# Moving the softplus series of dt from VectorE to GpSimd in a two-block kernel, with the quotient taken through a power

## The chip, the cores and the metric

The kernel runs on one core of one Trainium2 chip. The metric is the device time of one launch in microseconds. Before the change three timed runs gave a median of 1166.14 us (1164.15 to 1167.24).

The engines have short names in the profile: PE is TensorE, PEld its weight loads, DVE is VectorE, ACT is ScalarE, POOL is GpSimd and SP is SyncE. Each engine works through its own queue in order; semaphores tie the queues together.

## The reference, cut to what matters

Two blocks of a transformer for 256 tokens of width 1024 in float32. The first block is a short convolution mixer, a latent attention mixer and two squared-relu layers. The second has a gated layer, a hybrid mixer (a state space part beside chunked attention) and a second gated layer. The change touches the step size of the state space part alone:

```python
dt = jax.nn.softplus(dt_raw.astype(jnp.float32) + dt_bias.astype(jnp.float32))
a = -jnp.exp(a_log.astype(jnp.float32))
...
xdt = (xf * dt[..., None]).reshape(bsz, nc, CHUNK, n_groups, m, hd)
a_cs = jnp.cumsum((dt * a).reshape(bsz, nc, CHUNK, n_groups, m), axis=2)
```

There are 16 heads, so dt is 256 tokens by 16 heads. On the chip that is 128 partitions by 32 columns (two tiles of 128 tokens, 16 heads each).

The kernel takes softplus(x) as max(x, 0) + log(1 + e) with e = exp(-|x|), and log(1 + e) as 2 (z + z^3/3 + ... + z^19/19) with z = e / (2 + e).

## The kernel before, in words

**Weights.** Every product takes its weights in slabs of 128 partitions by at most 2048 columns, through a ring of four places. SP loads a slab into `raw` as soon as the slab four before it has been split. ACT rounds it to `weight_hi` (`round_slab`, recorded at L591). DVE subtracts to get `weight_lo` (`split_slab`, recorded at L956); both of its inputs lie in SBUF. PE multiplies high by high, low by high and high by low (`up_product`, L1441 to L1443, 48 matmuls of 256 columns for a slab).

**The stage of the change.** It is the first part of the hybrid mixer in the second block. PE first makes v and dt (three slabs, `HV`), then six slabs of the convolution input (`HX`, j = 0 to 5), then four of queries and keys (`HQK`). The orders are written out by hand, one list for each engine:

- DVE takes dt_raw from PSUM and adds the bias (L1284), makes -|x| (L1286, L1287), splits one slab (the fourth of HX), works through the series (L1290 to L1304), and then for j = 0 to 5 does three taps of the causal convolution (L1313, six instructions: one input in PSUM, one in SBUF) and splits the slab four ahead. At j = 4 it also copies the running sums out.
- ACT takes exp(-|x|) (L850) and exp(a_log) (L852), then for each j the first tap with its bias (L869), the rounding of a slab, and the Silu of the convolution before it (L858, `conv_out`). After the last Silu it loads another function table and takes the exponentials of the running sums (L888, `decays`).
- PE, after the product of HX slab 3, waits for `adt`, the product of dt and a, which the series ends in. It then makes the running sums with four small matmuls (L1850 to L1853), and goes on with HX slabs 4 and 5 and the first slab of queries and keys. Then it waits for the fourth Silu and for `decays` before the transposes of L1870.
- POOL issues small loads (L535 to L537, and one of L487), and then waits for the running sums (L543).

Every small instruction of DVE and POOL whose result the next one reads goes through `then`: it counts up a semaphore and the engine waits for it. POOL's own work elsewhere is of the same kind: `root` (L492, L493) adds a constant and raises to the power -0.5 with `half_neg`, on one column, or on two at one place.

The values of dt and adt lie in `dt_work`, 10 rows of 32 columns inside `arena`, the name that the trace shows. dt itself is read by DVE at L1335.

Of the kernel before, what the change touches and what calls it, by code (L numbers as in the profile page):

```python
# [26 lines left out]
ALU = mybir.AluOpType  # L27
AX_X = mybir.AxisListType.X

P = 128  # L30
TOKENS = 256
TILES = TOKENS // P
# [20 lines left out]
SSD_HEADS, SSD_HD, SSD_GROUPS = 16, 64, 2  # L53
# [43 lines left out]
def two_blocks(nc, t, consts, out):  # L97
# [43 lines left out]
    with ExitStack() as ctx:  # L141
        def sb(name, shape, dt=F32):
            return ctx.enter_context(nc.sbuf_tensor(name, shape, dt))
# [32 lines left out]
        half_neg = sb("half_neg", [P, 1])  # L176
# [17 lines left out]
        def take(n, *dims):  # L194
            a = arena[:, at[0]:at[0] + n]
            at[0] += n
            if len(dims) == 2:
                a = a.rearrange("p (a b) -> p a b", a=dims[0])
            return a
# [26 lines left out]
        dt_work = take(10 * 32, 10, 32)  # L226
# [25 lines left out]
        class Sems:  # L252
# [5 lines left out]
            def __getitem__(self, n):  # L258
# [12 lines left out]
        hy = Sems("hy", "rows tap0 conv xbc dt_abs dt_exp adt qk_out v_out cum_ps cum_out cum_rows cum_kept cum_wide0 cum_wide1 decays "  # L271
                        "xs_ps xs_out y_skip xdt hank bias_ready cb_ps cb_act cb seg exp seg_w y_ps off_ps off_taken "
                        "y_sum z_gate y_gated sumsq rstd y_n y_ps_t y_hi y_lo")
# [11 lines left out]
        def spread(v, n):  # L285
            return v.rearrange("(a n) -> a n", a=1).to_broadcast([P, n])
# [4 lines left out]
        def heads(a, n=8):  # L291
            return a.rearrange("p (h d) -> p h d", h=n)

        def per_head(a, n=8):

            return a.unsqueeze(2).to_broadcast([P, n, SSD_HD])
# [165 lines left out]
        def _(pool):  # L462
# [22 lines left out]
            def norm_rows(b, *pairs):  # L485
                for dst, v, n in pairs:
                    pool.dma_start(dst, spread(v, n)).then_inc(norm[b]["rows"], 16)  # L487
# [49 lines left out]
            pool.dma_start(dskip_row, spread(t["d_skip_2"][0], SSD_HEADS)).then_inc(hy["rows"], 16)  # L537
            pool.wait_ge(norm[5]["tok"], 2 * TILES)
            norm_rows(6, (gain[:, :], t["ffn2_norm_2"][0], D))

            pool.wait_ge(hy["rows"], 64)
            pool.wait_ge(hy["cum_rows"], 1)
            pool.dma_start(cum_kept, rows[0:TILES * SSD_HEADS, :]).then_inc(hy["cum_kept"], 16)  # L543
            for g in range(4):
                tile, h = g // 2, g % 2
# [398 lines left out]
        def _(dve):  # L944
            steps = [0]
            vec = nc.vector

            def then(ins):

                steps[0] += 1  # L950
                ins.then_inc(dve_step, 1)
                dve.wait_ge(dve_step, steps[0])
# [5 lines left out]
            def split_slab(m):  # L958

                if m >= N_SLABS:  # L960
                    return
                dve.wait_ge(hi_done, m + 1)
                w = width[m]
                rest(weight_lo[:, m % RING, 0:w], raw[:, m % RING, 0:w], weight_hi[:, m % RING, 0:w])\
                    .then_inc(lo_done, 1)
# [85 lines left out]
            for c in range(SC_CHUNKS):  # L1051
# [8 lines left out]
                for back in (1, 2):  # L1060
                    for f in range(CT):
                        o = f * TOKENS
                        row = ROW_SC + (SC_TAPS - 1 - back) * KD + CT * c + f
                        ins = vec.scalar_tensor_tensor(
                            tmp_c[:, o + back:o + TOKENS], tmp_b[:, o:o + TOKENS - back], cols[:, row:row + 1],
                            tmp_c[:, o + back:o + TOKENS], ALU.mult, ALU.add)
# [209 lines left out]
            split_slab(HV + 1 + RING)  # L1276


            x_dt, neg_abs, e_dt, z_dt, z2_dt, series, dt, _, adt, exp_a = [dt_work[:, i, :] for i in range(10)]
            minus_adt = z_dt  # L1280
            dve.wait_ge(hy["rows"], 64)
            for tile in range(TILES):
                sl = slice(tile * SSD_HEADS, (tile + 1) * SSD_HEADS)
                ins = vec.tensor_tensor(x_dt[:, sl], acc[:, 2 * tile + 1, VDT // 2 - SSD_HEADS:VDT // 2], dtb_row, ALU.add)  # L1284
# [1 line left out]
            then(vec.tensor_scalar(neg_abs, x_dt, -1.0, None, ALU.mult))  # L1286
            vec.tensor_tensor(neg_abs, neg_abs, x_dt, ALU.min).then_inc(hy["dt_abs"], 1)  # L1287
            split_slab(HV + 2 + RING)
            dve.wait_ge(hy["dt_exp"], 2)
            then(vec.tensor_scalar(z_dt, e_dt, 2.0, None, ALU.add))  # L1290
            then(vec.reciprocal(z_dt, z_dt))
            then(vec.tensor_tensor(z_dt, z_dt, e_dt, ALU.mult))
            then(vec.tensor_tensor(z2_dt, z_dt, z_dt, ALU.mult))
            then(vec.tensor_scalar(series, z2_dt, 1.0 / 19, None, ALU.mult))
            for k in (17, 15, 13, 11, 9, 7, 5, 3):
                then(vec.scalar_tensor_tensor(series, series, 1.0 / k, z2_dt, ALU.add, ALU.mult))
            then(vec.scalar_tensor_tensor(series, series, 1.0, z_dt, ALU.add, ALU.mult))
            then(vec.tensor_scalar(dt, x_dt, 0.0, None, ALU.max))
            then(vec.scalar_tensor_tensor(dt, series, 2.0, dt, ALU.mult, ALU.add))
            for tile in range(TILES):  # L1300
                sl = slice(tile * SSD_HEADS, (tile + 1) * SSD_HEADS)
                ins = vec.tensor_tensor(minus_adt[:, sl], dt[:, sl], exp_a[:, 0:SSD_HEADS], ALU.mult)
            then(ins)
            vec.tensor_scalar(adt, minus_adt, -1.0, None, ALU.mult).then_inc(hy["adt"], 1)  # L1304

            for j in range(6):
                cy, ps = (tmp_a, tmp_b)[j % 2], up[j % 4]
                dve.wait_ge(hy["tap0"], CT * (j + 1))
                for back in (1, 2, 3):
                    for f in range(CT):  # L1310
                        o = f * TOKENS
                        row = ROW_XBC + (XBC_TAPS - 1 - back) * XT + CT * j + f
                        ins = vec.scalar_tensor_tensor(  # L1313
                            cy[:, o + back:o + TOKENS], ps[:, o:o + TOKENS - back], cols[:, row:row + 1],
                            cy[:, o + back:o + TOKENS], ALU.mult, ALU.add)
# [15 lines left out]
            for g in range(4):  # L1331
                tile, h = g // 2, g % 2
                dve.wait_ge(hy["xs_out"], g + 1)
                hd = tile * SSD_HEADS + 8 * h
                vec.tensor_tensor(heads(xdt[:, tile, h * HALF:(h + 1) * HALF]), heads(acc[:, g, :]),  # L1335
                                  per_head(dt[:, hd:hd + 8]), ALU.mult).then_inc(hy["xdt"], 1)
                if g == 1:
                    dve.wait_ge(hy["decays"], 1)
                    dve.wait_ge(hy["xdt"], 2)
                    vec.tensor_tensor(heads(xdt_end, SSD_HEADS), heads(xdt[:, 0, :], SSD_HEADS),  # L1340
                                      per_head(dt_work[:, 7, 0:SSD_HEADS], SSD_HEADS), ALU.mult).then_inc(hy["cb"], 1)
# [34 lines left out]
            for p in range(4):  # L1376
                g, tile = p % 2, p // 2
# [31 lines left out]
            for g in range(4):  # L1409
                tile, f = g // 2, g % 2  # L1410
# [580 lines left out]
```

## Time and profile before

| | |
|---|---|
| median of three runs | 1166.14 us (1164.15 to 1167.24) |
| the profiled execution, its own time | 1164.75 us |
| its span in the trace | 1162.9 us |
| PE busy | 1135.6 us, 98% of the span |
| DVE busy | 656.1 us, 56% |
| ACT busy | 514.4 us, 44% |
| POOL busy | 55.9 us, 5% |
| granted TensorE clock, mean | 0.995 of full |

Times in the trace are counted from the start of the span. The length of a matmul is from its start to the end of its drain, so starts are the better measure of PE's pace: in this stage they lie 0.12 us apart. Lines of a timeline merge instructions of one kind that follow each other (x6 is six of them, and the length is that of all). In square brackets stands the idle time of the engine before the line, and what ended it.

### The profile page before, as it was taken

Reading aid. Unit: us, or ns where it says so; the run is one execution under the profiler, and the core shown is the slowest. Engines: PE = TensorE matmul, PEld = TensorE weight load, DVE = VectorE, ACT = ScalarE, POOL = GpSimd, SP = SyncE. Lnnn points to the kernel's source line nnn. Section 1 sums busy time; section 2 is a strip of 40 time slices with the busy share of each in tenths; the row PEclk is TensorE's granted clock in tenths of the full one; section 3 lists DMA queues with packets and bytes.
Section 4 is the critical chain, followed back from the end, with each engine's and each line's share of the span. In section 5 each row is a group of like instructions: output and inputs, shape, how many; then the busy total and the mean of one; then the engine's idle time right before and its main releaser. Section 6 shows DMA issues by size and latency. Waiting matters only on the chain.

```text
span 1162.9 us, 18298 instructions
## 1 busy us (share of the span) xinstructions
PE 1135.6 (98%) x7542; PEld 1020.1 (88%) x7542; DVE 656.1 (56%) x736; ACT 514.4 (44%) x581; POOL 55.9 (5%) x103
## 2 busy tenths in 40 slices
PE   9999999999999999999999999999989999999997
PEld 7897999998886799999879999988987778999996
DVE  4756655555764664555474454446966765544553
ACT  4533444434445244444443434344636734443342
POOL 1000000000200000000010000001041011000000
PEclk9999999999999999999999999999989999999999
DMA  9654665554651476565544555565664153555641
GB/s 336 231 193 148 210 204 178 187 183 129 179 176 43 145 235 186 182 209 181 162 145 144 201 188 173 181 183 176 199 190 162 56 181 127 175 183 184 205 141 50
DMA packets 141627, 201.77 MB, mean 174 GB/s; under 512 B 9432, under 2 KB 119232, under 8 KB 141584
## 3 DMA queue, kind: packets, MB, share of 16 engines
q1 hardware_dynamic: 138208, 190.27, 50.7%
q0 software_dynamic: 3376, 10.90, 3.0%
q8 instruction: 31, 0.51, 0.2%
q14 instruction: 12, 0.10, 0.0%
HBM read 200.08 MB, written 1.06 MB: 173 GB/s over the span
## 4 chain that ended last, share of the span: by engine, by line
PE 86%; DVE 7%; ACT 3%; DMA 2%; issue 1%; POOL 1%; SPq 0%; DVEq 0%; POOLq 0%; ACTq 0%
PE up L1441 15%; PE up L1443 15%; PE up L1442 15%; PE acc L1474 11%; PE acc L1475 11%; PE acc L1477 11%; DVE weight_lo L956 2%; DMA raw<-in_sc_w_in 2%; ACT weight_hi L591 1%; PE acc L1547 1%; PE up L1518 1%; PE up L1791 1%; PE up L1529 1%; PE up L1463 1%; PE up L1467 1%
## 5 line engine op out<-in xcount | busy, mean ns | idle before, releaser
L956 DVE TENSOR_TENSOR weight_lo<-raw,weight_hi 128x2048 fp32r<-128x2048 f32 (+4 forms) x206 | 414.3, 2017 | 310.5 <-ACT weight_hi L591 310.3
L1441 PE MATMUL up<-xh,weight_hi 128*128 128x256 f32 x1548 | 440.8, 285 | 2.2 <-ACT cols L591 1.1
L591 ACT ACTIVATE weight_hi<-raw 128x2048 fp32r<-128x2048 f32 (+4 forms) x206 | 347.5, 1694 | 214.1 <-PE acc L1477 120.0
L1443 PE MATMUL up<-xh,weight_lo 128*128 128x256 f32 x1548 | 438.4, 283 | 0.0
L1442 PE MATMUL up<-xl,weight_hi 128*128 128x256 f32 x1548 | 438.4, 283 | 0.0
L1441 PEld LDWEIGHTS up<-xh,weight_hi 128*128 128x128 f32 x1548 | 297.4, 192 | 6.2 <-issue 1.7
L1442 PEld LDWEIGHTS up<-xl,weight_hi 128*128 128x128 f32 x1548 | 297.4, 192 | 2.7 <-issue 0.7
L1443 PEld LDWEIGHTS up<-xh,weight_lo 128*128 128x128 f32 x1548 | 297.2, 192 | 0.0
L1474 PE MATMUL acc<-weight_hi,hh 128*128 128x512 f32 x480 | 187.6, 391 | 0.6 <-DVE hl L956 0.6
L1475 PE MATMUL acc<-weight_lo,hh 128*128 128x512 f32 x480 | 187.5, 391 | 0.0
L1477 PE MATMUL acc<-weight_hi,hl 128*128 128x512 f32 x480 | 150.3, 389 | 0.0
L1477 PEld LDWEIGHTS acc<-weight_hi,hl 128*128 128x128 f32 x480 | 90.1, 188 | 19.2
L1474 PEld LDWEIGHTS acc<-weight_hi,hh 128*128 128x128 f32 x480 | 90.3, 188 | 18.8 <-issue 2.0
L1475 PEld LDWEIGHTS acc<-weight_lo,hh 128*128 128x128 f32 x480 | 90.3, 188 | 17.0
L678 ACT ACTIVATE tmp_a<-up 128x512 f32<-128x512 f32 x32 | 19.2, 599 | 120.7 <-PE up L1443 115.9
L1097 DVE TENSOR_TENSOR tmp_b<-tmp_a 128x512 f32<-128x512 f32 x32 | 22.2, 693 | 65.5 <-ACT tmp_a L678 65.5
L714 ACT ACTIVATE tmp_a<-up 128x512 f32<-128x512 f32 x22 | 13.2, 598 | 97.3 <-PE up L1443 93.2
L1474 PE MATMUL acc<-weight_hi,xh 128*128 128x256 f32 (+1 forms) x152 | 51.5, 339 | 1.3 <-DVE xl L956 1.3
L1475 PE MATMUL acc<-weight_lo,xh 128*128 128x256 f32 (+1 forms) x152 | 50.7, 333 | 0.0
L591 ACT ACTIVATE xh<-up 128x512 fp32r<-128x512 f32 (+1 forms) x43 | 22.7, 551 | 55.2 <-PE up L1529 43.0
L1477 PE MATMUL acc<-weight_hi,xl 128*128 128x256 f32 (+1 forms) x152 | 46.1, 333 | 0.0
L956 DVE TENSOR_TENSOR xl<-up,xh 128x512 fp32r<-128x512 f32 (+1 forms) x43 | 25.2, 630 | 27.5 <-ACT xh L591 27.2
(223 smaller groups left out, 856.7 us busy)
## 6 DMA issues: line engine op xcount, KB each, us to landing
raw<-in_ff_w SPq DMA_DIRECT2D x64, 1024.0 KB, 5.3
raw<-in_ffn_w_gate SPq DMA_DIRECT2D x22, 1024.0 KB, 5.4
raw<-in_ffn_w_up SPq DMA_DIRECT2D x22, 1024.0 KB, 5.4
raw<-in_ffn_w_down SPq DMA_DIRECT2D x44, 512.0 KB, 4.6
raw<-in_w_in SPq DMA_DIRECT2D x14, 1024.0 KB, 5.6
raw<-in_sc_w_in SPq DMA_DIRECT2D x11, 1024.0 KB, 7.5
raw<-in_w_out SPq DMA_DIRECT2D x6, 1024.0 KB, 5.0
raw<-in_sc_w_out SPq DMA_DIRECT2D x4, 1024.0 KB, 5.2
```

What stands on the lines that cost most here:

```text
L591: return nc.scalar.activation(dst, src, ACT.Copy, **kw)
L678: nc.scalar.activation(tmp_a[:, :], up[par][:, :], ACT.Relu).then_inc(q["relu"], 1)
L714: nc.scalar.activation(tmp_a[:, :], up[2 * par][:, :], ACT.Silu).then_inc(q["gate"], 1)
L956: return vec.tensor_tensor(dst, whole, high.bitcast(F32), ALU.subtract)
L1097: vec.tensor_tensor(tmp_b[:, :], tmp_a[:, :], tmp_a[:, :], ALU.mult).then_inc(q["squared"], 1)
L1441: mm(dst, w_h, xh[:, x_tile + k, :], start=first and k == 0, stop=False)
L1442: mm(dst, w_h, xl[:, x_tile + k, :], start=False, stop=False)
L1443: ins = mm(dst, w_l, xh[:, x_tile + k, :], start=False, stop=last and k == k_tiles - 1)
L1463: mm(dst, w_h[k], xh[:, k, :], start=k == 0, stop=False)
L1474: mm(d, s_h, h, start=first, stop=False, **open_group)
L1475: mm(d, s_h, l, start=False, stop=False, **open_group)
L1477: ins = mm(d, s_l, h, start=False, stop=last, **open_group)
```

## The change

The series of dt and its products go from DVE's queue to POOL's, where they stand behind the small loads and in front of the wait for the running sums. [...] The reciprocal of 2 + e becomes (2 + e)^-0.5, multiplied in twice. DVE keeps the bias and -|x|. PE's wait for `adt` stays where it is; DVE gets a wait for it ahead of the first product that reads dt (L1335).

```diff
             pool.wait_ge(norm[5]["tok"], 2 * TILES)
             norm_rows(6, (gain[:, :], t["ffn2_norm_2"][0], D))
+
+            x_dt, _, e_dt, z_dt, z2_dt, series, dt, _, adt, exp_a = [dt_work[:, i, :] for i in range(10)]
+            minus_adt = z_dt
+            gps = nc.gpsimd
+            pool.wait_ge(hy["dt_exp"], 2)
+            then(gps.tensor_scalar(z2_dt, e_dt, 2.0, None, ALU.add))
+            then(gps.tensor_tensor(z2_dt, z2_dt, half_neg[:, :].to_broadcast([P, 32]), ALU.pow))
+            then(gps.tensor_tensor(z_dt, e_dt, z2_dt, ALU.mult))
+            then(gps.tensor_tensor(z_dt, z_dt, z2_dt, ALU.mult))
+            then(gps.tensor_tensor(z2_dt, z_dt, z_dt, ALU.mult))
+            then(gps.tensor_scalar(series, z2_dt, 1.0 / 19, None, ALU.mult))
+            for k in (17, 15, 13, 11, 9, 7, 5, 3):
+                then(gps.tensor_scalar(series, series, 1.0 / k, None, ALU.add))
+                then(gps.tensor_tensor(series, series, z2_dt, ALU.mult))
+            then(gps.tensor_scalar(series, series, 1.0, None, ALU.add))
+            then(gps.tensor_tensor(series, series, z_dt, ALU.mult))
+            then(gps.tensor_scalar(series, series, 2.0, None, ALU.mult))
+            then(gps.tensor_scalar(dt, x_dt, 0.0, None, ALU.max))
+            then(gps.tensor_tensor(dt, series, dt, ALU.add))
+            for tile in range(TILES):
+                sl = slice(tile * SSD_HEADS, (tile + 1) * SSD_HEADS)
+                then(gps.tensor_tensor(minus_adt[:, sl], dt[:, sl], exp_a[:, 0:SSD_HEADS], ALU.mult))
+            gps.tensor_scalar(adt, minus_adt, -1.0, None, ALU.mult).then_inc(hy["adt"], 1)
 
             pool.wait_ge(hy["rows"], 64)
             pool.wait_ge(hy["cum_rows"], 1)
...
             vec.tensor_tensor(neg_abs, neg_abs, x_dt, ALU.min).then_inc(hy["dt_abs"], 1)
             split_slab(HV + 2 + RING)
-            dve.wait_ge(hy["dt_exp"], 2)
-            then(vec.tensor_scalar(z_dt, e_dt, 2.0, None, ALU.add))
-            then(vec.reciprocal(z_dt, z_dt))
-            then(vec.tensor_tensor(z_dt, z_dt, e_dt, ALU.mult))
-            then(vec.tensor_tensor(z2_dt, z_dt, z_dt, ALU.mult))
-            then(vec.tensor_scalar(series, z2_dt, 1.0 / 19, None, ALU.mult))
-            for k in (17, 15, 13, 11, 9, 7, 5, 3):
-                then(vec.scalar_tensor_tensor(series, series, 1.0 / k, z2_dt, ALU.add, ALU.mult))
-            then(vec.scalar_tensor_tensor(series, series, 1.0, z_dt, ALU.add, ALU.mult))
-            then(vec.tensor_scalar(dt, x_dt, 0.0, None, ALU.max))
-            then(vec.scalar_tensor_tensor(dt, series, 2.0, dt, ALU.mult, ALU.add))
-            for tile in range(TILES):
-                sl = slice(tile * SSD_HEADS, (tile + 1) * SSD_HEADS)
-                ins = vec.tensor_tensor(minus_adt[:, sl], dt[:, sl], exp_a[:, 0:SSD_HEADS], ALU.mult)
-            then(ins)
-            vec.tensor_scalar(adt, minus_adt, -1.0, None, ALU.mult).then_inc(hy["adt"], 1)
-
             for j in range(6):
...
                 hd = tile * SSD_HEADS + 8 * h
+                if g == 0:
+                    dve.wait_ge(hy["adt"], 1)
                 vec.tensor_tensor(heads(xdt[:, tile, h * HALF:(h + 1) * HALF]), heads(acc[:, g, :]),
```

## Rows read from the trace of the kernel before

**Rows 1.** The page: busy time of each engine, then the chain's shares.

```profile
PE 1135.6 (98%) x7542; PEld 1020.1 (88%) x7542; DVE 656.1 (56%) x736; ACT 514.4 (44%) x581; POOL 55.9 (5%) x103
...
PE 86%; DVE 7%; ACT 3%; DMA 2%; issue 1%; POOL 1%; SPq 0%; DVEq 0%; POOLq 0%; ACTq 0%
```

**Rows 2.** Timeline of DVE from 813 us: start, length, line, operation [idle before].

```profile
813.23 2.29 DVE L956 TENSOR_TENSOR weight_lo<-raw,weight_hi 128x2048 fp32r<-128x2048 f32 x1 [2.21 <-ACT weight_hi L591]
815.44 0.17 DVE L1290 TENSOR_SCALAR arena<-arena 128x32 f32<-128x32 f32 x1
...
819.58 2.68 DVE L1313 SCALAR_TENSOR_TENSOR tmp_a<-up,cols,tmp_a 128x255 f32<-128x255 f32 x6
822.17 2.28 DVE L956 TENSOR_TENSOR weight_lo<-raw,weight_hi 128x2048 fp32r<-128x2048 f32 x1
...
843.92 2.66 DVE L1313 SCALAR_TENSOR_TENSOR tmp_b<-up,cols,tmp_b 128x255 f32<-128x255 f32 x6
```

**Rows 3.** Timeline of ACT, at both ends of the stage.

```profile
811.18 0.20 ACT L852 ACTIVATE arena<-arena 128x16 f32<-128x16 f32 x1
...
839.15 1.02 ACT L869 ACTIVATE tmp_b<-up,cols 128x256 f32<-128x256 f32 x2 [1.84 <-PE up L1443]
...
846.61 0.63 ACT L858 ACTIVATE arena<-tmp_b 128x512 f32<-128x512 f32 x1 [4.11 <-DVE tmp_b L1313]
847.26 1.28 ACT L888 ACT_TABLE_LOAD   x1
```

**Rows 4.** Timeline of PE, at the wait for adt and at the transposes.

```profile
826.12 0.28 PE L1443 MATMUL up<-xh,weight_lo 128*128 128x256 f32 x1
826.33 0.41 PE L1850 MATMUL acc<-cst,arena 128*32 128x128 f32 x2
...
848.90 3.65 PE L1870 MATMUL acc<-cst,arena 128*128 128x128 f32 x16 [4.02 <-ACT arena L888]
```

**Rows 5.** Stages: us, busy of PE, PEld, DVE, ACT, POOL, granted clock, DMA share, GB/s.

```profile
845.00:849.00 4.00, 0.10 (x1) 0.14 (x2) 3.74 (x5) 2.36 (x4) 0.10 (x1) 0.82 0.88 250
849.00:852.00 3.00, 3.00 (x15) 3.00 (x16) 0.86 (x1) 3.00 (x5) 0.39 (x1) 0.50 0.64 152
852.00:855.00 3.00, 3.00 (x18) 3.00 (x17) 2.90 (x4) 1.10 (x3) 3.00 (x2) 0.60 0.70 213
```

**Rows 6.** Timeline of POOL: two columns, then one column, then its wait.

```profile
308.11 0.73 POOL L493 TENSOR_TENSOR rstd<-rstd,half_neg 128x2 f32<-128x2 f32 x1
...
589.76 0.19 POOL L525 TENSOR_TENSOR rstd<-mean_sq 128x1 f32<-128x1 f32 x1
590.04 0.22 POOL L492 TENSOR_SCALAR rstd<-rstd 128x1 f32<-128x1 f32 x1
590.35 0.57 POOL L493 TENSOR_TENSOR rstd<-rstd,half_neg 128x1 f32<-128x1 f32 x1
...
844.55 0.55 POOL L543 DMA_DIRECT2D cum_kept<-rows  x1 [52.65 <-DVE rows L1325]
```

**Rows 7.** POOL's four wide products: count, shortest/median/longest in ns, starts, form.

```profile
L548 POOL TENSOR_TENSOR normed<-normed,arena x4: 1034/1530/2726, 851.6 to 857.3; 128x512 f32<-128x512 f32 x4
```

**Rows 8.** Timeline of DVE, then of POOL, at 928 us.

```profile
928.22 4.49 DVE L956 TENSOR_TENSOR weight_lo<-raw,weight_hi 128x2048 fp32r<-128x2048 f32 x2
...
928.53 2.07 POOL L492 TENSOR_SCALAR rstd<-sumsq 128x1 f32<-128x1 f32 x1 [23.34 <-ACT bias L926]
930.68 2.46 POOL L493 TENSOR_TENSOR rstd<-rstd,half_neg 128x1 f32<-128x1 f32 x1
```

**Rows 9.** Timeline of DVE beside the one-column work of POOL in rows 6.

```profile
588.93 1.41 DVE L1015 SCALAR_TENSOR_TENSOR x_tok<-acc,mean_var,gain 128x512 f32<-128x512 f32 x2
590.38 0.75 DVE L1020 SCALAR_TENSOR_TENSOR x_tok<-x_tok,rstd,bias 128x512 f32<-128x512 f32 x1
```

**Rows 10.** Two products of DVE over 1024 columns, the first beside POOL's L548.

```profile
854.74 1.69 DVE L1340 TENSOR_TENSOR arena<-arena 128x1024 f32<-128x1024 f32 x1
...
927.09 1.22 DVE L1399 TENSOR_TENSOR normed<-normed,arena 128x1024 f32<-128x1024 f32 x1
```

More of the change, by code:

```diff
@@ L1276, in _ @@
             split_slab(HV + 1 + RING)
-            x_dt, neg_abs, e_dt, z_dt, z2_dt, series, dt, _, adt, exp_a = [dt_work[:, i, :] for i in range(10)]
-            minus_adt = z_dt
+            x_dt, neg_abs, dt = dt_work[:, 0, :], dt_work[:, 1, :], dt_work[:, 6, :]
             dve.wait_ge(hy["rows"], 64)
```

## The prediction

> **What bounds the kernel now.** I read the page first. PE is busy for 98% of the span and makes up 86% of the chain that ended last [rows 1], so a saving on DVE counts only where PE waits for DVE. I then read the timelines of the stage. From 815.44 us on DVE has no idle time: the series takes until 819.58, and six rounds of taps and a split follow, the last taps starting at 843.92 [rows 2]. A round is 2.6 us of taps and 2.2 us of split, 4.8 us (822.17 less 819.58, and the split's 2.28 less the overlap of starts). PE needs 48 matmuls x 0.12 = 5.8 us for a slab. DVE began late and catches up, but not wholly: the last taps end at 846.6, the last Silu follows at once, then a table load of 1.28 us [rows 3], and PE, idle for 4.02 us, starts its transposes at 848.90 [rows 4]. The stages show a second cost. The mean clock from 845 to 849 us is 0.82, so it fell to half (1.2 GHz) at about 847.6, 2.7 us after PE fell idle at 844.9; it is 0.50 until 852 and 0.60 from 852 to 855, so it rose at about 854.4 [rows 5]. PE worked from 848.9 to 854.4 at half speed, 5.5 us for 2.75 us of work.
>
> **What the removal is worth.** DVE loses 19 instructions, 819.58 - 815.44 = 4.14 us [rows 2]. I replayed the stage from 815.44 with the rows' lengths. The taps then start earlier, and from j = 3 on they wait for PE. PE's slab 5 is done where it was, and the first tap behind it starts at 839.15 as before [rows 3]. It lasts 1.0 us, the DVE taps until 842.7, Silu, table and exponential (0.6 + 1.28 + 0.2) until 844.9, and PE starts near 845.1 instead of 848.90: 3.8 us. Its idle time shrinks to some 0.2 us, so the clock has no idle time to fall in, which gives back 2.75 us. Together 6.6 us, if `adt` is there in time.
>
> **When adt is needed.** PE ends slab 3 at 826.12 + 0.12 = 826.24 and goes on at 826.33 [rows 4]: there is no wait now, since DVE's adt is there at 819.6. Behind that wait in PE's queue stand the running sums, slabs 4 and 5 and everything after. PE is the bound, so each us of lateness is paid in full.
>
> **What POOL needs.** The input is there when ACT's L852 ends, 811.4 [rows 3]; POOL has been idle since its small loads, 52.65 us in all [rows 6]. It gets 30 instructions: one addition, the power, and 28 more (13 with a constant, 15 with two tensors).
> - A small one of one column takes 0.19 us (two tensors) or 0.22 (constant), and the next starts 0.09 us later, 590.04 less 589.76 less 0.19 [rows 6]. For the columns I take the shortest L548, 1.034 us for 512 [rows 7]: (1.034 - 0.19)/511 = 1.65 ns a column, 0.05 us for 31. So 0.33 or 0.35 us each from start to start, 28 of them 15 x 0.33 + 13 x 0.35 = 9.5 us.
> - The power takes 0.57 us for one column and 0.73 for two [rows 6]: 0.16 us a column. For 32 that is 0.57 + 31 x 0.157 = 5.4 us. No row has more than two. Bounds: 0.6 us, if the second column's price is not repeated; 12.3 us, if each column costs what the first does above an addition, 0.19 + 32 x 0.38. I take 5.4, the only slope that a row shows.
>
> Undisturbed, adt comes at 811.4 + 0.35 + 5.4 + 9.5 = 826.7, almost in time. But POOL is disturbed. Two starts of DVE's split (both inputs in SBUF) fall at 928.22 and 930.42. POOL's addition, started at 928.53, lasts 2.07 us instead of 0.22 and ends at 930.60, just behind the first split; the power, started at 930.68, lasts 2.46 instead of 0.57 and ends 0.43 behind the second [rows 8]. So while a split runs POOL's next instruction stands, and one gets through for each. Beside L1015, with one input in PSUM and one in SBUF like the taps L1313, four of POOL's keep their 0.19 to 0.57 us [rows 6, 9]: the taps let POOL through. (The Trainium skill, SBUF — State Buffer, "Who interferes with whom", says this too: a VectorE instruction contends with a GpSimd one that reads SBUF when it has two SBUF inputs, not when it has one. The trace agrees: 2.07 against 0.22 us.)
>
> So each round of 4.8 us gives POOL the 2.6 us of taps: seven instructions, and the eighth stands until the split ends. Without the series DVE's splits lie at 813.2 to 815.4, 818.0 to 820.2, 822.8 to 825.0, 827.6 to 829.8 and 832.4 to 834.6. The power runs from 811.75 to 817.2, over the first of them. I take its reads as done by then. Three more start before 818.0, the fourth stands until 820.4; seven and one until 825.2; seven and one until 830.0; the last eight need 2.7 us, so adt comes at 832.7, or at 834.9 if the last falls into the split at 832.4. I take 833.8, a stall S of 7.5 us (6.5 to 8.7). Without the splits it would be 0.5 us.
>
> **The clock again.** An idle time of 7.5 us is longer than the 4.02 us in which it fell before. If it falls after 2.7 us again, that is at 829.0. Before, it stood at half for 6.8 us, 5.5 of them behind PE's new start. If the 6.8 us are what repeats, PE works at half from 833.8 to 835.8 and loses 1.0; if the 5.5, it loses 2.75. I take 2.0.
>
> **The sum.** PE starts its transposes S + 2.0 later than the 6.6 us of gain would have it: 7.5 + 2.0 - 6.6 = +2.9 us (bounds with S and the clock: 6.5 + 1.0 - 6.6 = +0.9 and 8.7 + 2.75 - 6.6 = +4.9). What follows the transposes hangs on PE and moves with it. Other edits at nothing: DVE's new wait at L1335 lies behind running sums that already need adt; behind POOL's new work stands L543, which waits for the same sums; with DVE earlier the slabs are loaded earlier, never later. The series' DVE time would have been hidden only where DVE has idle time, and that is not the case here.
>
> **Rivals.**
> 1. *A power whose price hardly grows with the columns* (0.6 us). It ends at 812.4; with the same blocking, adt comes at 827.7 to 830.0: a stall of 1.5 to 3.7 us, the clock lost or not: 6.6 less that, -5 to -0.2 us, middle 1162.6. Against it speaks the 0.16 us between one and two columns.
> 2. *A costly power, the other side: slower.* At 12.3 us it ends at 824.0. Nine instructions get through until 830.0, seven and one until 834.8, the other eleven run free, since DVE then waits for PE: 838.6, S = 12.4, and with 0 to 2.75 us of clock +5.8 to +8.6, middle 1173.3. It decides (over 0.3%) from S + clock = 10.1 us, a power of about 7 us.
> 3. *The power holds DVE's split back.* L1340, started 0.44 us after a wide product of POOL, takes 1.69 us instead of the 1.22 of L1399 [rows 10]: DVE waited 0.47. If the power keeps the way to SBUF for all its 5.4 us, the split of 813.23 starts at 817.1, DVE gains nothing, and the same count gives adt at 835.0: S = 8.8, +2.6 to +5.0, middle 1169.9. Against it: L1020, two inputs in SBUF, started 0.03 us after a power of one column and took its full-speed 0.75 us [rows 6, 9], so one column is not held through the arithmetic; with 32 no row tells. The Trainium skill, SBUF — State Buffer, "SBUF: two separate sides", says that the first to start gets the shared pair for the whole instruction. By that rule this rival is the forecast. Its sum would be +3.8 us where mine is +2.9.
> 4. *The splits don't hold 32-column instructions up as they did one-column ones.* adt at 826.7, S = 0.5, -6.1 us, 1160.0. Against: rows 8, twice.
>
> **How the numbers follow.** A difference under 0.3% (3.5 us) can't be told from none here. Chances: forecast 0.45, rival 1 0.13, rival 2 0.18, rival 3 0.20, rival 4 0.04. Slower by over 3.5 us come all of rival 2, half of rival 3 and a fifth of the forecast: 0.37. Faster come half of rival 1 and all of rival 4, and a little for what I overlook: 0.13. The rest, 0.50, is within 0.3%. The profiled execution took 1164.75 us for a span of 1162.9; the sum makes it 1167.7. The median of the runs lies 1.4 above it, so I predict 1166.1 + 2.9 = 1169.0. The range leaves out the tails of rivals 1 and 2: 1162.5 to 1174.0.
>
> **What the profile after would show.** The first taps of DVE at 815.5 (right) or 819 (rival 3). One POOL power of 128x32 near 5.4 us, the others near 0.25 us with some of 2 us under the splits. PE idle before L1850 for some 7 us, released by POOL, and a clock at half in that wait; no idle time of 4 us before L1870. The prediction is wrong if the power is far from 5.4 us, if small instructions of POOL have another price at 32 columns than at one, or if the taps hold POOL up too.

## The result, and the profile after

The changed kernel takes 1172.07 us (median; 1169.19 to 1172.81) against 1166.14 before, five runs each: a ratio of 1.0048, 95% interval 1.0031 to 1.0065. It is slower by half a per cent. The prediction said 1169.0, within 1162.5 to 1174.0, and gave "within 0.3%" the highest chance; the measured time lies in the range and past that bound, on the side that had 0.37.

The first view is the page of the changed kernel: busy time of each engine, then the chain's shares, as in [rows 1].

```profile
PE 1136.9 (97%) x7542; PEld 1021.2 (87%) x7542; DVE 652.6 (56%) x717; ACT 513.5 (44%) x581; POOL 77.0 (7%) x133
...
PE 86%; DVE 4%; ACT 3%; POOL 3%; DMA 2%; issue 1%; SPq 0%; DVEq 0%; POOLq 0%; ACTq 0%
```

DVE's share of the chain fell from 7% to 4% and POOL's rose from 1% to 3%. POOL got 21 us of busy time for the 3.5 us that DVE lost. In the listings that follow, the lines of the changed kernel are numbered 23 higher in ACT's part and 5 to 23 higher in DVE's and PE's.

POOL's timeline shows what the 21 us are (start, length, line, operation):

```profile
812.43 0.31 POOL L545 TENSOR_SCALAR arena<-arena 128x32 f32<-128x32 f32 x1 [21.16 <-ACT arena L875]
812.82 5.46 POOL L546 TENSOR_TENSOR arena<-arena,half_neg 128x32 f32<-128x32 f32 x1
818.36 0.26 POOL L547 TENSOR_TENSOR arena<-arena 128x32 f32<-128x32 f32 x1
818.70 0.25 POOL L548 TENSOR_TENSOR arena<-arena 128x32 f32<-128x32 f32 x1
819.02 2.33 POOL L549 TENSOR_TENSOR arena<-arena 128x32 f32<-128x32 f32 x1
...
824.00 2.21 POOL L552 TENSOR_SCALAR arena<-arena 128x32 f32<-128x32 f32 x1
...
828.77 2.23 POOL L552 TENSOR_SCALAR arena<-arena 128x32 f32<-128x32 f32 x1
...
833.22 2.51 POOL L561 TENSOR_TENSOR arena<-arena 128x16 f32<-128x16 f32 x2
835.82 0.29 POOL L562 TENSOR_SCALAR arena<-arena 128x32 f32<-128x32 f32 x1
```

And DVE's beside it, as in [rows 2]:

```profile
814.17 2.29 DVE L979 TENSOR_TENSOR weight_lo<-raw,weight_hi 128x2048 fp32r<-128x2048 f32 x1 [2.20 <-ACT weight_hi L614]
816.38 2.68 DVE L1318 SCALAR_TENSOR_TENSOR tmp_a<-up,cols,tmp_a 128x255 f32<-128x255 f32 x6
818.98 2.28 DVE L979 TENSOR_TENSOR weight_lo<-raw,weight_hi 128x2048 fp32r<-128x2048 f32 x1
...
823.77 2.29 DVE L979 TENSOR_TENSOR weight_lo<-raw,weight_hi 128x2048 fp32r<-128x2048 f32 x1
...
833.37 2.28 DVE L979 TENSOR_TENSOR weight_lo<-raw,weight_hi 128x2048 fp32r<-128x2048 f32 x1
846.35 2.68 DVE L1318 SCALAR_TENSOR_TENSOR tmp_a<-up,cols,tmp_a 128x255 f32<-128x255 f32 x6 [10.70 <-ACT tmp_a L892]
```

The taps start right behind the split of 814.17, as wanted. The power takes 5.46 us. Each of POOL's three instructions of 2.2 to 2.3 us began within 0.25 us of the start of a split and ended just behind it; the two of L561 are one more case, 2.51 us for both with the split of 833.37 beside them. The same operations take 0.25 to 0.3 us elsewhere. Behind the split of 833.37 DVE has 10.70 us of idle time: it waits, through ACT, for PE. PE's timeline and the stages with their clock show why (us, busy of PE, PEld, DVE, ACT, POOL, granted clock, DMA share, GB/s):

```profile
827.08 0.28 PE L1450 MATMUL up<-xh,weight_lo 128*128 128x256 f32 x1
836.16 0.64 PE L1857 MATMUL acc<-cst,arena 128*32 128x128 f32 x2 [8.81 <-POOL arena L562]
...
857.12 1.94 PE L1877 MATMUL acc<-cst,arena 128*128 128x128 f32 x16 [0.34 <-ACT arena L911]
```

```profile
830.00:834.00 4.00, 0.00 (x0) 0.00 (x0) 3.93 (x8) 0.73 (x2) 3.34 (x9) 0.58 0.63 175
834.00:838.00 4.00, 1.84 (x8) 1.45 (x9) 1.65 (x1) 0.00 (x0) 2.02 (x2) 0.50 0.74 206
838.00:842.00 4.00, 4.00 (x24) 4.00 (x25) 0.00 (x0) 0.00 (x0) 0.00 (x0) 0.64 0.64 219
```

The wait of 4.02 us before the transposes [rows 4] has become 0.34, and 16 transposes take 1.94 us instead of 3.65. In its place PE waits 8.81 us for POOL's last instruction, and the clock is at half from 830.6 (0.58 is 3.4 of 4 us at half) to 840.9 (0.64 is 2.9 of 4). PE works in the last 4.7 us of that and loses 2.35.

**A ruler for the stage.** The starts of a run differ by 1 to 3 us before the stage is reached, so I measure within it, in the one profiled execution of each kernel: from the start of the second exponential on ACT to the start of the first product behind the transposes (`bc_t`). Before and after:

```profile
859.00 0.59 PE L1877 MATMUL up<-arena 128*128 128x256 f32 x2
```

```profile
812.14 0.20 ACT L875 ACTIVATE arena<-arena 128x16 f32<-128x16 f32 x1
...
864.64 0.59 PE L1884 MATMUL up<-arena 128*128 128x256 f32 x2
```

Before it is 859.00 - 811.18 [rows 3] = 47.8 us, after it is 864.64 - 812.14 = 52.5. The stage costs 4.7 us more.

### The profile page after: what moved, and what is told of

The parts are those of the page before. It is cut to its first block, busy times and chain, and to the rows that moved or that the text cites. A ratio compares the mean times of both kernels' runs of the same rounds, so it can differ in the third digit from the quotient of the medians.

```text
span 1168.5 us, 18310 instructions
## 1 busy us (share of the span) xinstructions
PE 1136.9 (97%) x7542; PEld 1021.2 (87%) x7542; DVE 652.6 (56%) x717; ACT 513.5 (44%) x581; POOL 77.0 (7%) x133
## 4 chain that ended last, share of the span: by engine, by line
PE 86%; DVE 4%; ACT 3%; POOL 3%; DMA 2%; issue 1%; SPq 0%; DVEq 0%; POOLq 0%; ACTq 0%
PE up L1448 15%; PE up L1450 15%; PE up L1449 15%; PE acc L1481 11%; PE acc L1482 11%; PE acc L1484 11%; DMA raw<-in_sc_w_in 2%; PE acc L1554 1%; DVE weight_lo L979 1%; PE up L1525 1%; ACT weight_hi L614 1%; PE up L1536 1%; PE up L1798 1%; PE up L1470 1%; PE up L1474 1%
## 5 line engine op out<-in xcount | busy, mean ns | idle before, releaser
L1484 PE MATMUL acc<-weight_hi,xl 128*128 128x256 f32 (+1 forms) x152 | 46.1, 333 | 0.0
```

The lines of the kernel that those rows point to most:

```text
L1484: ins = mm(d, s_l, h, start=False, stop=last, **open_group)
```

## The experiments

Theory A is the prediction's: every us that adt comes behind PE's slab 3 is paid, with the clock that falls in the wait, and nothing else of the change costs. Its rivals stand in the expectations. All kernels but e4, e6 and e9 are edits of the changed kernel. "Stage" is the ruler above; "stall" is PE's wait for adt. The kernel before was run again beside each group of kernels, and each ratio is to those runs: their median was 1165.68 us beside e1 to e4, 1164.90 beside e5 to e8 and 1166.33 beside e9. The kernels e1 and e3 leave out the quotient and so don't compute dt; e2 leaves out terms of the series and computes it more coarsely.

| run | time, us | ratio to before, 95% interval | stall, us | stage, us |
|---|---|---|---|---|
| before | 1166.14 | | 0 | 47.8 |
| changed | 1172.07 | 1.0048 (1.0031 to 1.0065) | 8.81 | 52.5 |
| e1 no power | 1160.14 | 0.9944 (0.9927 to 0.9960) | 1.35 | 43.0 |
| e2 two terms | 1160.21 | 0.9946 (0.9930 to 0.9963) | 0.62 | 42.3 |
| e3 both short | 1161.02 | 0.9946 (0.9927 to 0.9965) | 0 | 41.6 |
| e4 ladder | 1165.93, one run | | 0 | 47.8 |
| e5 sums late | 1159.22 | 0.9954 (0.9940 to 0.9969) | 0 | 41.0 |
| e6 splits late, series on DVE | 1160.96 | 0.9962 (0.9949 to 0.9975) | 0 | 41.6 |
| e7 reciprocal on DVE | 1161.32 | 0.9963 (0.9949 to 0.9978) | 0.94 | 42.6 |
| e8 splits moved | 1165.64 | 1.0003 (0.9993 to 1.0012) | 2.97 | 46.1 |
| e9 sums late, series on DVE | 1165.73 | 1.0003 (0.9992 to 1.0013) | 0 | 46.4 |

The ruler and the ratios differ by up to 2 us, in both directions: e1 gains 4.8 us on the ruler and some 6.5 by its ratio, e6 gains 6.2 and some 4.4. So the order of e1, e2, e3, e6 and e7 among themselves is read from stall and stage, and the times show only that all five are faster than the kernel before.

**e1: no power.** The quotient is left out.

```diff
-            then(gps.tensor_scalar(z2_dt, e_dt, 2.0, None, ALU.add))
-            then(gps.tensor_tensor(z2_dt, z2_dt, half_neg[:, :].to_broadcast([P, 32]), ALU.pow))
+            then(gps.tensor_scalar(z2_dt, e_dt, 1.0, None, ALU.mult))
+            then(gps.tensor_tensor(z2_dt, z2_dt, half_neg[:, :].to_broadcast([P, 32]), ALU.mult))
```

> The quotient is left out: the first instruction and the power on GpSimd become plain multiplications, the other 28 instructions stay. Theory A (lateness: every us that adt comes after TensorE's slab 3 is paid, and nothing else of the change costs): the GpSimd chain loses 5.2 us of 5.46, but the splits of VectorE still stop it four times, so adt comes 5 to 7 us earlier than in the changed kernel. TensorE's stall falls from 8.8 us to 2 to 4 us, and the clock falls for a short time or not at all. Gain over the kernel before 6.6 less 2 to 4 less 0 to 2.4: 1160 to 1166 us, middle 1163. Theory B (the early start of the taps brings nothing, because the table load, the rounding or the loads set the transposes; the stall is all that counts): the kernel before plus the stall, 1168 to 1170 us.

The stall fell to 1.35 us, below the 2 to 4 that theory A expected, and the time to 1160.14, at the lower end of its range. adt came 7.5 us sooner, where 5 to 7 was expected, for 5.2 us of work less: three of POOL's instructions were held back by a split, and not four as I had written. Theory B, which wanted 1168 to 1170 us, is ruled out.

**e2: two terms.** Six of the eight middle terms of the series are left out.

```diff
-            for k in (17, 15, 13, 11, 9, 7, 5, 3):
+            for k in (5, 3):
```

> The power stays, six of the eight middle terms of the series are left out (k = 5 and 3 stay), so GpSimd runs 18 instructions instead of 30. Theory A: counted with seven free instructions for each round of taps and one held back by each split, adt comes about 8 us earlier than in the changed kernel, the stall is 0 to 1.5 us, the clock does not fall there, and the time is 6.6 less the stall below the kernel before: 1159.5 to 1161.5 us. Theory B: 1166 to 1168 us.

The stall is 0.62 us and the time 1160.21, as theory A has it.

**e3: both.** The two edits together.

> Both cuts together: no power and two of eight middle terms. adt is far ahead of TensorE's slab 3. Theory A: no stall there at all, the transposes start 3.8 us earlier than in the kernel before and at full clock, 1159.5 us (-6.6). It is the ceiling of what leaving the series off VectorE can bring. Theory B: equal to the kernel before, 1166 us.

adt is there 4.9 us ahead of PE. The stage takes 41.56 us where it took 47.82 before, 6.3 less; the prediction had 6.6 for a kernel without a stall. The median, 1161.02 us, is 1.5 above what was expected. The five runs of this kernel spread from 1157.89 us (mean clock 0.999) to 1162.64 (0.994), which is told below.

**e4: the ladder.** The kernel before, with unused work on POOL at the start.

```diff
+            then(nc.gpsimd.memset(ladder[:, :], 2.5))
+            for n in (1, 2, 4, 8, 16):
+                then(nc.gpsimd.tensor_tensor(ladder[:, 0:n], ladder[:, 0:n], half_neg[:, :].to_broadcast([P, n]), ALU.pow))
+            for n in (1, 16, 32):
+                then(nc.gpsimd.tensor_tensor(ladder[:, 0:n], ladder[:, 0:n], ladder[:, 32:32 + n], ALU.mult))
+                then(nc.gpsimd.tensor_scalar(ladder[:, 0:n], ladder[:, 0:n], 1.5, None, ALU.add))
```

> The kernel before with a ladder of instructions on GpSimd at the start of the program, where VectorE and GpSimd are idle: powers over 1, 2, 4, 8 and 16 columns, then a product and an addition over 1, 16 and 32 columns. If the price of the power is 0.57 us and 0.157 us for each further column: 0.57, 0.73, 1.04, 1.67, 2.92 us. If only the long one has such a slope, the short ones lie flatter. The small instructions: 0.19, 0.22, 0.24 us (product) and 0.22, 0.25, 0.27 us (addition) by the slope of the 512-column product; the changed kernel's rows say 0.25 and 0.29 at 32 columns. The time of the whole kernel is not changed by more than 3 us, as the ladder lies before the first load is used.

POOL's timeline of e4, four of the five powers and the small instructions of 32 columns:

```profile
1.82 0.56 POOL L479 TENSOR_TENSOR ladder<-ladder,half_neg 128x1 f32<-128x1 f32 x1
2.46 0.70 POOL L479 TENSOR_TENSOR ladder<-ladder,half_neg 128x2 f32<-128x2 f32 x1
4.33 1.63 POOL L479 TENSOR_TENSOR ladder<-ladder,half_neg 128x8 f32<-128x8 f32 x1
6.05 2.90 POOL L479 TENSOR_TENSOR ladder<-ladder,half_neg 128x16 f32<-128x16 f32 x1
...
12.22 0.25 POOL L481 TENSOR_TENSOR ladder<-ladder 128x32 f32<-128x32 f32 x1
12.55 0.31 POOL L482 TENSOR_SCALAR ladder<-ladder 128x32 f32<-128x32 f32 x1
```

The power over four columns took 1.02 us. With the 5.46 us of the changed kernel the power goes as 0.4 us and 0.16 us a column from 1 to 32. A line through two points, one and two columns, was a good guide to 32. The addition at 32 columns takes 0.3 us and not 0.27. VectorE was not idle through the whole ladder, as I had written: it subtracted two half slabs from 9.14 to 11.69 us, and the addition over one column (1.14 us, started at 9.30) and the product over 16 (1.24 us, started at 10.53) ran beside them, so these two say nothing of the price.

**e5: sums late.** All the arithmetic of the changed kernel. PE waits for adt behind slab 5, not 3. DVE's copies of the running sums move with it, from j = 4 to j = 5, and stand in front of the split; ACT waits for them before its exponentials.

```diff
+            act.wait_ge(hy["cum_rows"], 1)
...
-                split_slab(HX + j + RING)
-                if j == 4:
+                if j == 5:
                     dve.wait_ge(hy["cum_ps"], 1)
...
+                split_slab(HX + j + RING)
...
-                if j == 3:
+                if j == 5:
                     pe.wait_ge(hy["adt"], 1)
```

> The changed kernel with all its arithmetic, but TensorE waits for adt and makes the running sums behind HX slab 5 instead of slab 3, and VectorE copies them out behind its last taps. Lateness alone (theory A): adt at some 24 us behind the second exponential still comes before TensorE's slab 5 ends (some 27.5 us behind it), so the 8.8 us of stall and the half clock are gone, and from the exponential to the products behind the transposes it takes 41.5 to 43 us instead of 52.5 (47.8 in the kernel before). Time 1159.5 to 1161.5 us. Theory C (the place does not matter, GpSimd's work itself slows VectorE and so the stage): still above 1166 us.

POOL's chain is as long as ever; its last instruction starts at 834.53 in this run, 23.7 us behind the exponential (23.7 in the changed kernel too). The end of POOL's chain and PE's timeline of e5, with no idle time at the sums and none before the transposes:

```profile
834.53 0.30 POOL L562 TENSOR_SCALAR arena<-arena 128x32 f32<-128x32 f32 x1
...
837.84 0.40 PE L1859 MATMUL acc<-arena,cst 128*128 128x16 f32 x2
...
844.37 1.91 PE L1878 MATMUL acc<-cst,arena 128*128 128x128 f32 x16
```

The time is 1159.22 us, ratio 0.9954 (0.9940 to 0.9969): faster than both kernels. So POOL's work as such costs nothing that shows; the place of the wait did (e9 is the control). Theory C is ruled out.

**e6: splits late.** The kernel before, with three splits behind the last taps.

```diff
-                split_slab(HX + j + RING)
+                if j < 3:
+                    split_slab(HX + j + RING)
+                if j == 5:
+                    split_slab(HX + 3 + RING)
+                    split_slab(HX + 4 + RING)
+                    split_slab(HX + 5 + RING)
```

> The kernel before, the series on VectorE as it was, but the splits of j = 3, 4 and 5 (slabs that TensorE wants later) stand behind the last taps. If what the change could have brought at most is the 3.8 us of idle time before the transposes and the clock that falls in it, then taking 4.4 us of other work off VectorE's way to the last taps brings the same: 41.5 to 42.5 us from the exponential to the products behind the transposes, 1159.5 to 1161 us, without any work moved to GpSimd. If the series itself is special (its chain of small waits), 1164 to 1166 us.

The stage is 41.6 us, as in e3: the same gain comes from two splits (j = 3 and 4, 4.4 us) taken out of the way of DVE's last taps as from the series (4.14 us). What mattered was DVE's time ahead of its last taps, not what it was spent on.

**e7: reciprocal on DVE.** The changed kernel with a true reciprocal, made by DVE ahead of a split; POOL has 27 small instructions and no power.

```diff
+            dve.wait_ge(hy["dt_exp"], 2)
+            then(vec.tensor_scalar(dt_work[:, 4, :], dt_work[:, 2, :], 2.0, None, ALU.add))
+            vec.reciprocal(dt_work[:, 3, :], dt_work[:, 4, :]).then_inc(hy["dt_exp"], 1)
             split_slab(HV + 2 + RING)
...
-            pool.wait_ge(hy["dt_exp"], 2)
-            then(gps.tensor_scalar(z2_dt, e_dt, 2.0, None, ALU.add))
-            then(gps.tensor_tensor(z2_dt, z2_dt, half_neg[:, :].to_broadcast([P, 32]), ALU.pow))
-            then(gps.tensor_tensor(z_dt, e_dt, z2_dt, ALU.mult))
-            then(gps.tensor_tensor(z_dt, z_dt, z2_dt, ALU.mult))
+            pool.wait_ge(hy["dt_exp"], 3)
+            then(gps.tensor_tensor(z_dt, e_dt, z_dt, ALU.mult))
```

> The changed kernel, but the sum 2 + e and its reciprocal are made by VectorE in the 2 us in which it waits for a rounding, and GpSimd runs 27 small instructions without a power. Theory A: GpSimd starts 0.7 us later than with the power and needs 5.5 us and three instructions less; adt comes within 0.7 us of TensorE's slab 3. Stall 0 to 1 us, 1160 to 1161.5 us. If the number of instructions and not the power is what makes adt late, the stall stays at 3 us or more and the time at 1163 or above.

Stall 0.94 us, stage 42.6, 1161.32 us, near the upper end of what was expected. The reciprocal of 32 columns takes DVE 0.35 us, in idle time: 1.23 us of waiting for the rounding are left behind it. The power takes POOL 5.46.

**e8: splits moved.** POOL's list is untouched; two of DVE's splits lie elsewhere.

```diff
-                split_slab(HX + j + RING)
+                for late in {0: (0,), 3: (1, 2, 3), 4: (4,), 5: (5,)}.get(j, ()):
+                    split_slab(HX + late + RING)
```

> The changed kernel, GpSimd's work as it is, but VectorE's splits of j = 1 and 2 stand behind the taps of j = 3, so that one split instead of four lies over GpSimd's small instructions. Theory A with the splits as the cause of the lateness: three instructions of GpSimd lose their 2 us, adt comes at about 18.2 us behind the second exponential instead of 24, and the stall falls from 8.8 to about 3 us; 1162 to 1165 us. Rival (the instructions of 2.2 us have another cause, as loads or the code of GpSimd): three of them stay, adt and the stall stay where they were, 1170 us.

From POOL's timeline of e8, the one small instruction that was held, and the end of the chain:

```profile
818.87 2.34 POOL L549 TENSOR_TENSOR arena<-arena 128x32 f32<-128x32 f32 x1
...
829.22 0.52 POOL L561 TENSOR_TENSOR arena<-arena 128x16 f32<-128x16 f32 x2
829.82 0.29 POOL L562 TENSOR_SCALAR arena<-arena 128x32 f32<-128x32 f32 x1
```

adt came 18.1 us behind the exponential, where 18.2 was expected; the three other long instructions are gone with the splits. The stall is 2.97 us as expected. The time, 1165.64, missed the 1162 to 1165. A part of that is the clock, which fell after all. The stages show it at half for 3.4 us (3.0 in the first stage and 0.4 in the second), all of it PE at work: 1.7 us, which I had left out. With it the stage is still 1.7 us shorter than before, and the median of ten runs is not; that part is open.

```profile
830.00:834.00 4.00, 3.83 (x20) 3.63 (x21) 3.96 (x5) 0.57 (x2) 0.12 (x1) 0.63 0.00 0
834.00:838.00 4.00, 4.00 (x34) 4.00 (x33) 3.57 (x2) 0.00 (x0) 0.00 (x0) 0.95 0.94 263
```

**e9: the control of e5.** The edit of e5 on the kernel before.

> The control of the run before with the running sums behind HX slab 5: the same edit on the kernel before, with the series on VectorE. Theory A: VectorE, busy without a gap until its last taps, sets the transposes and not the place of the sums; the 4 us of idle time before the transposes stay (3 to 4 us, as the sums now lie in it or beside it), from the exponential to the products behind the transposes it takes 46.5 to 48 us, time 1164 to 1167 us. Rival (the late sums are a gain by themselves, and the move adds nothing): 1159 to 1161 us.

PE still waits 3.67 us before the transposes, and the ratio is 1.0003 (0.9992 to 1.0013): the late sums bring nothing by themselves that ten runs show. On the ruler the stage is 1.4 us shorter than before, just below the 46.5 that was expected, as the clock stood at half for a shorter time (the 16 transposes take 2.44 us, not 3.65). Even if that is counted, 5.4 of e5's 6.8 us are left: its gain needs both, the series off DVE and the wait later.

## Why the prediction came out as it did

**The gain of the removal.** Predicted 6.6 us, 3.8 of idle time and 2.75 of clock. e3 shows 6.3: the transposes start 3.7 us sooner on the ruler, and from there to the first product it takes 7.5 us instead of 10.1. e5, where PE has no idle time at all, shows 6.8. The replay held.

**The power.** 5.4 us predicted, 5.46 measured. Rivals 1 and 2 fall, and e4 shows the slope in between.

**The blocking.** Shown by e8. Rival 4 falls.

**The power and DVE's split (rival 3).** The split of 814.17 starts under the power and takes its usual 2.29 us, and the taps follow at 816.38. With 32 columns the power doesn't hold DVE back, so rival 3 falls with its mechanism, although its numbers lie nearer than mine: adt at 835.0 is 23.8 us behind the exponential (24.0 measured, 22.6 forecast), and its stall of 8.8 us is the measured one. The rule of the Trainium skill (SBUF — State Buffer, "SBUF: two separate sides"), that the first to start keeps the shared pair for the whole instruction, doesn't hold for this power: 5.46 us of power, and no delay of the split under it.

**The step that was mis-sized is the stall S.** I put it at 7.5 us (6.5 to 8.7), and it was 8.81. adt came 24.0 us behind the start of the exponential; I had 22.6. The power started 0.68 us behind that start, where I had 0.57 (811.75 less 811.18); a small instruction with a constant takes 0.29 + 0.08 us, not 0.35; so two and not three instructions fit between the power and the next split, which then held the third. That split and the next two each held one instruction. At the far end the second half of L561 fell into the split of 833.37. I had seen that this could happen (834.9) and averaged over it. With splits of 2.2 us over a chain of 0.36 us steps, 0.1 us of lateness anywhere becomes 2 us or nothing, so the mean of the two ends was a value that by my own count could not come out.

**The clock.** 2.0 us predicted, 2.35 measured, but neither of the two readings that 2.0 was the middle of came true: the clock stood at half for 10.3 us, not 6.8, and for 4.7 us behind PE's new start, not 5.5. That the middle was close is luck.

**The sum** with the measured terms is 8.8 + 2.35 - 6.3 = 4.9 us against 4.7 on the ruler, at the upper bound of the prediction's +0.9 to +4.9. The medians differ by 5.9, twice the +2.9 of the forecast and outside these bounds; the range up to 1174.0 held the time because it left room for a costlier power, which did not come.

**What is left.** The profiled execution grew by 5.6 us in span, the stage by 4.7. Behind the stage both kernels need 303.9 us (1162.9 - 859.00 and 1168.5 - 864.64), so the rest lies ahead of it. In the changed kernel's profile the clock also fell some 20 us ahead of the stage, in a wait of 2.0 us that both kernels have, and not in that of before. Before, then after:

```profile
792.00:796.00 4.00, 2.51 (x21) 2.51 (x22) 3.80 (x4) 0.79 (x2) 0.00 (x0) 1.00 1.02 279
```

```profile
792.00:796.00 4.00, 3.14 (x15) 3.14 (x16) 3.00 (x2) 0.28 (x1) 0.00 (x0) 0.63 1.01 296
```

The changed kernel was 0.6 us ahead of before at 788 us and 0.95 behind when the stage began. The profiles have three such places outside the stage, near 590, 790 and 970 us. The kernel before and e5 fell in none of them, the changed kernel in the second alone, e3 and e6 in all three (clock of 0.91 to 0.93 over 580 to 600, 780 to 800 and 960 to 980 us). e4 and e6, edits of the kernel before, fell at 790 us too, so this fall doesn't need the change. One of them costs some 1.5 us: e3 takes 305.3 us behind the stage and not 303.9. That is also what the spread of e3's runs looks like. The medians differ by 5.9 us. Whether the remaining 1.2 is chance of this kind, or whether the changed kernel meets such falls more often, is not settled: its five runs have mean clocks of 0.991 to 0.994.

## What to carry to other kernels

Moving work to an idle engine frees the busy one, but the result gets a new arrival time: time the first reader of the result too, and move the wait behind work that is ready. Here the same 30 instructions cost half a per cent with PE's wait behind slab 3 and saved as much with it behind slab 5 (ratios 1.0048 and 0.9954), while the later wait alone, without the move, brought nothing that the times show (1.0003). Count a chain of small GpSimd instructions by the gaps between VectorE's instructions with two SBUF inputs, not by their sum, and quote both ends where a step may fall on either side of one. And before moving work away, look whether the busy engine does something that nobody waits for: three splits moved in its own queue (e6) brought about the same (0.9962).

## What the runs showed of the hardware that was not expected

- A power over 32 columns on GpSimd costs 5.46 us, a product 0.25; 0.16 us against about 0.002 us a column.
- A power of 32 columns on GpSimd that started 1.35 us ahead of a VectorE split did not delay it, and was not delayed by it (5.46 and 2.29 us, both undisturbed). A product or an addition of 32 columns that started beside a split took 2.2 to 2.3 us instead of 0.25 to 0.3. Why the power is different is not shown.
- The clock fell to half in waits of very different length: in the changed kernel 3.3 us into a wait of 8.81 us, in e8 just after work had resumed behind a wait of 2.97 us, and in some executions in or just behind a wait of 2.0 us, in others not. Runs of one kernel (e3) differ by 4.7 us between a mean clock of 0.999 and of 0.994, more than many changes bring: a profile that is compared with another should first be compared in the stretches that neither change touches.
